# Cross-attention scores of the later blocks as three fp32r products, with the queries' lower parts on GpSimd

## The chip, the core and the metric

The kernel runs on one core of a Trainium2 chip. Its time is the device time of one execution in microseconds, as the median of the runs shown. Its engines are named as in the profile: PE is TensorE (matmuls; PEld are its weight loads), DVE is the Vector engine, ACT is ScalarE, POOL is GpSimd and SP is SyncE, which here only issues transfers.

## What is computed

One layer of a hybrid decoder for 1024 prompt tokens and 64 sample tokens (8 sequences of 8), all in float32: a feed-forward half step, a mixer of a recurrent and a sliding-window attention part, a cross attention over 256 memory tokens, a second feed-forward half step, and a final norm. The part that matters here is the cross attention, with 4 heads of width 256:

```
def cross_attend(h, mk, mv, w_cq, w_co):
    q = (h @ w_cq).reshape(n, t, X_HEADS, X_HEAD_DIM)
    s = jnp.einsum('nthd,nmhd->nhtm', q, mk) * (X_HEAD_DIM ** -0.5)
    p = jax.nn.softmax(s, axis=-1)
    o = jnp.einsum('nhtm,nmhd->nthd', p, mv).reshape(n, t, D_MODEL)
    return o @ w_co
```

The prompt tokens share one memory (`mk`, `mv`), each sample sequence has its own.

## The kernel before

Activations lie feature-major in SBUF: a tensor `[128, 8, T]` holds 1024 features as 8 tiles of 128 partitions, for T = 1088 tokens, the 64 of the samples first. Most products are made as three fp32r products: each operand is split into an upper part, rounded to fp32r, and a lower part, the operand less its upper part, and `three` (line 905) issues upper x upper, upper x lower and lower x upper into one PSUM bank. The products inside the attention are plain fp32 matmuls, each of which the trace shows as two instructions.

The weights of the five plain projections come as 27 pairs of tiles, of 128 x 1024 each. SP loads them (`load_pairs`), POOL splits each tile into an upper and a lower part in eight pieces of 128x256 (`split_plain`, lines 805 and 791 to 792), one pair after the other in `split_pairs` (line 835), and may overwrite `w_hi` and `w_lo` of a pair only when PE is through with the pair before it. Pairs 15 to 18 are the mixer's output projection, 19 to 22 the queries (`PAIR_CQ` = 19), 23 to 26 the cross attention's output projection (`PAIR_CO` = 23). POOL's program is one queue: line 882 runs the splits of pairs 18 to 26 in one loop, and after it the first weights of the second feed-forward part.

The cross attention runs in 8 steps, one for each block b of 128 prompt tokens and, at the same time, for sample sequence b. The order within a step is written out by hand on each engine, and semaphores tie them together:

- PE, `x_step(b)` (line 1483): the scores of block b+1 (`x_scores`, line 1425, into banks 0 and 1), the turn of block b's probabilities (`x_turn`, line 1453), the sample scores of b+1 (`y_scores`, line 1437), the turn of the sample's (`y_turn`), and the products with the values (`x_weigh`, lines 1471 and 1479). Step 0 is written out ahead of the loop, with `x_scores(0)` and `x_scores(1)` in the last tile of the query projection.
- DVE, `x_step(b)` (line 2878): the row maximum of b+1 (`x_soft`, lines 2855 to 2860), the copies of block b+2's queries into operands for PE (`x_stage`: `qs_b` on line 2850 and `xq_b` on line 2851, which raises `xq_st`), the normalization of b+1 (`x_norm`, lines 2864 to 2869), and the result of b out of PSUM (`x_take`).
- ACT, `x_step(b)` (line 1973): the turned probabilities out of PSUM, the exponentials of b+1 (`x_exps`, lines 1961 to 1964), and `y_s`, the sample's result, out of PSUM.
- SP loads the sample keys and values (`load_keys`, `load_values`), two sequences ahead, and the weights of pair 23 between the first of these.
- POOL has no part in a step. The split of pair 23 falls among the steps, because its weights come then.

`x_scores(b)` waits for `xq_st` at b+1 and `x_exp` at b+1. The keys `mem_kT` (128 x 8 x 256, fp32) were made by the memory projection long before.

Of the kernel before, what the change touches and what calls it, by code (L numbers as in the profile page):

```python
# [22 lines left out]
F32 = mybir.dt.float32  # L23
F32R = mybir.dt.float32r
ALU = mybir.AluOpType
ACT = mybir.ActivationFunctionType
AX_X = mybir.AxisListType.X

P = 128
D = 1024  # L30
KT = D // P
SEQ = 1024
NS, LS = 8, 8
TS = NS * LS
# [9 lines left out]
NB = SEQ // WIN  # L44
KVH = 2
GRP = NH // KVH
NM = 256
XH = 4
# [6 lines left out]
NC = len(CH)  # L55
# [65 lines left out]
PAIR_IN, PAIR_KV, PAIR_OUT, PAIR_CQ, PAIR_CO, PAIRS = 0, 7, 15, 19, 23, 27  # L121
# [84 lines left out]
def build(nc, t_in, t_out):  # L206
    ctx = ExitStack()
    with ctx:
        def sem(name):
            return ctx.enter_context(nc.semaphore(name))  # L210
# [5 lines left out]
        def at(name, shape, off, dt=F32):  # L216
            size = 4 * int(np.prod(shape[1:]))
            assert off % 32 == 0 and off + size <= LIMIT, (name, off, size)
            return nc.alloc_sbuf_tensor_at(name, shape, dt, offset=off)
# [120 lines left out]
        mem_kT = at("mem_kT", [P, KT, NM], P0 + M_G * ROW)  # L340
# [11 lines left out]
        def here(name, shape, dt=F32):  # L352
            off = cur[0]
            tns = at(name, shape, off, dt)
            cur[0] += -(-4 * int(np.prod(shape[1:])) // 32) * 32
            assert cur[0] <= (RS0 if off < RS0 else ACC0), name
            return tns
# [43 lines left out]
        xq = at("xq", [P, KT, T], P0 + 33792)  # L401
# [5 lines left out]
        qs_b = here("qs_b", [P, KT, 32])  # L407
# [8 lines left out]
        y_s = here("y_s", [P, NM])  # L416
        ck_T = [at("ck_T0", [P, KT, NM], ACC0), here("ck_T1", [P, KT, NM])]
        cv_n = [here(f"cv_n{s}", [P, 2, D]) for s in range(2)]

        y = at("y", [P, KT, T], A0)  # L420
        y_id = at("y_id", [P, P], A0 + KT * ROW)
# [2 lines left out]
        ps = ctx.enter_context(nc.psum_tensor("ps", [P, 8, 512], F32))  # L424
# [14 lines left out]
        memn_hi_done, memn_lo_done = sem("memn_hi_done"), sem("memn_lo_done")  # L439
# [62 lines left out]
        kw_hi_made = sem("kw_hi_made")  # L502
# [20 lines left out]
        ck_in = [sem(f"ck_in{s}") for s in range(2)]  # L523
        cv_in = [sem(f"cv_in{s}") for s in range(2)]
        xq_st = sem("xq_st")
        x_sc_mm, x_nmax, x_exp, x_p = sem("x_sc_mm"), sem("x_nmax"), sem("x_exp"), sem("x_p")
        x_turned = sem("x_turned")
        x_pt_mm, x_pt_ev, xp_ev = sem("x_pt_mm"), sem("x_pt_ev"), sem("xp_ev")
# [255 lines left out]
        def _(pool):  # L784
# [20 lines left out]
            def split_plain(s, p, hi=w_hi, lo=w_lo, less=0, both=True):  # L805
                pool.wait_ge(w_in[s], (p + 1) * 16)
                steps = Steps(pool, w_pool, p * (2 * KT // SHORT) + s * (KT // SHORT) - less * (KT // SHORT))
                split_short(w_raw[s], hi[s], lo[s], steps, w_split[s], both)
# [26 lines left out]
            def split_pairs(first, last, pair0, base, less=0):  # L835
                with pool.Fori(first, last) as p:
                    for s in range(2):
                        pool.wait_ge(w_mm[s], p * NC + (base - pair0 * NC))
                        split_plain(s, p, less=less)
# [31 lines left out]
            less = 2 * NB - 3  # L871
# [7 lines left out]
            for s in range(2):  # L879
                pool.wait_ge(w_mm[s], groups_before(PAIR_OUT + 1))  # L880
                split_plain(s, PAIR_OUT + 2, less=less)
            split_pairs(PAIR_OUT + 3, PAIRS, PAIR_OUT, 7 * NC, less=less)
            f = ffn["ffn2"]

            split_first(f)
# [2 lines left out]
            for c, (o, n) in enumerate(CH):  # L888
                for m in range(1, KT if c < NC - 1 else KT - 2):
                    i = c * KT + m  # L890
                    pool.wait_ge(sq_done, SQ0["final"] + i + 1)
                    if m == 1:
                        h = HALVES[0][0]
                        pool.tensor_tensor(acc[:, o:o + n], sq[:, h:h + n], sq[:, HALVES[1][0]:HALVES[1][0] + n],
                                           ALU.add).then_inc(sq_used, 2)
                    else:
                        h = HALVES[m % 2][0]
# [6 lines left out]
        def _(pe):  # L904
# [520 lines left out]
            def x_scores(b):  # L1425
                pe.wait_ge(xq_st, b + 1)
                pe.wait_ge(x_exp, b + 1)
                for h in range(XH):
                    for d in range(2):
                        pe.matmul(ps[:, h // 2, (h % 2) * NM:(h % 2 + 1) * NM], xq_b[:, 2 * h + d, :],  # L1430
                                  mem_kT[:, 2 * h + d, :], start=(d == 0), stop=(d == 1))

            def y_scores(b, half, s):
                pe.wait_ge(ck_in[s], half * 16 + 16)
                for h in range(XH):
                    for d in range(2):
                        ins = pe.matmul(ps[32 * h:32 * h + 32, 2, 0:NM], qs_b[:, 2 * h + d, :],
                                        ck_T[s][:, 2 * h + d, :], start=(d == 0), stop=(d == 1))
                ins.then_inc(x_sc_mm, 1)
# [7 lines left out]
            def x_turn(b, s):  # L1447

                pe.wait_ge(x_p, b + 1)
                pe.wait_ge(x_pt_ev, b + 1)  # L1450
                for h in range(XH):
                    for mt in range(2):
                        ins = pe.transpose(ps[:, 3 + mt, h * P:(h + 1) * P], xs_m[s][:, h, mt * P:(mt + 1) * P],
                                           x_id[:, :])
                ins.then_inc(x_turned, 1)

            def y_turn(b, s, after=True):

                if after:
                    pe.wait_ge(y_ev, b)  # L1460
                    back()
                for mt in range(2):
                    ins = pe.transpose(ps[:, 5, mt * P:(mt + 1) * P], ys_m[s][:, mt * P:(mt + 1) * P], x_id[:, :])
                ins.then_inc(x_pt_mm, 1)
# [17 lines left out]

            def x_step(b, half, s, more=True, after=True):
                if more:
                    x_scores(b + 1)
                x_turn(b, s)
                if more:
                    y_scores(b + 1, half + s, 1 - s)
                y_turn(b, s, after)
                x_weigh(b, half, s)  # L1490
# [34 lines left out]
        def _(act):  # L1525
# [432 lines left out]
            def x_exps(b, s):  # L1958
                act.wait_ge(x_nmax, b + 1)
                for h in range(XH):  # L1960
                    act.activation(xs_m[s][:, h, :], ps[:, h // 2, (h % 2) * NM:(h % 2 + 1) * NM], ACT.Exp,
                                   bias=xst[:, s, 1, h:h + 1], scale=XD ** -0.5, accum_out=xst[:, s, 2, h:h + 1])
                act.activation(ys_m[s][:, :], ps[:, 2, 0:NM], ACT.Exp, bias=yst[:, s * 4 + 1:s * 4 + 2],
                               scale=XD ** -0.5, accum_out=yst[:, s * 4 + 2:s * 4 + 3]).then_inc(x_exp, 1)
# [5 lines left out]
                    ps[:, 5, NM:2 * NM].rearrange("p (d w) -> p d w", d=2)[:, :, 0:P]  # L1970
                    .rearrange("p d (h w) -> p h d w", h=XH)[:, :, :, 0:LS], ACT.Copy)

            def x_step(b, s, more=True, after=True):

                act.wait_ge(x_turned, b + 1)
                act.activation(xp_T[:, :, :, :], ps[:, 3:5, :], ACT.Copy).then_inc(xp_ev, 1)
                act.wait_ge(x_pt_mm, b + 1)
                if after:
                    y_back(b - 1)
                act.activation(yp_T[:, :, :], ps[:, 5, 0:2 * P], ACT.Copy).then_inc(x_pt_ev, 1)  # L1980
                if more:
                    x_exps(b + 1, 1 - s)
                act.wait_ge(y_mm, b + 1)
                act.activation(y_s[:, :], ps[:, 5, NM:2 * NM], ACT.Copy).then_inc(y_ev, 1)

            act.sem_inc(x_exp, 1)
            act.sem_inc(x_pt_ev, 1)
            x_exps(0, 0)
            x_step(0, 0, after=False)
            x_step(1, 1)  # L1990
            with act.Fori(1, NB // 2 - 1) as i:
                x_step(i * 2, 0)
# [23 lines left out]
            for c, (o, n) in enumerate(CH):  # L2016
                for m in range(KT):
                    i, h = c * KT + m, HALVES[m % 2][0]
# [10 lines left out]
        def _(dve):  # L2029
# [815 lines left out]
            def xcol(b):  # L2845
                return bass.ds(b * P + TS, P)

            def x_stage(b):

                dve.tensor_copy(qs_b[:, :, :], xq[:, :, bass.ds(b * LS, 32)])  # L2850
                dve.tensor_copy(xq_b[:, :, :], xq[:, :, xcol(b)]).then_inc(xq_st, 1)

            def x_soft(b, s, steps):
                dve.wait_ge(x_sc_mm, b + 1)
                steps.mark(dve.tensor_reduce(xst[:, s, 0, :], ps[:, 0:2, :].rearrange("p a (h w) -> p (a h) w", w=NM),
                                             AX_X, ALU.max))
                steps.done(dve.tensor_reduce(yst[:, 4 * s:4 * s + 1], ps[:, 2, 0:NM], AX_X, ALU.max))
                dve.tensor_scalar(xst[:, s, 1, :], xst[:, s, 0, :], -(XD ** -0.5), None, ALU.mult)
                dve.tensor_scalar(yst[:, 4 * s + 1:4 * s + 2], yst[:, 4 * s:4 * s + 1], -(XD ** -0.5), None,
                                  ALU.mult).then_inc(x_nmax, 1)  # L2860
# [12 lines left out]
            def x_take(b):  # L2873
                dve.wait_ge(x_pv_mm, b + 1)
                take_out(xq[:, :, xcol(b)], ps[:, 6:8, :].rearrange("p a (k w) -> p (a k) w", w=P))\
                    .then_inc(x_o_ev, 1)

            def x_step(b, s, more=True, stage=True):
                if more:
                    steps = Steps(dve, x_own, (b + 1) * X_STEPS)  # L2880
                    x_soft(b + 1, 1 - s, steps)
                    if stage:
                        x_stage(b + 2)
                    x_norm(b + 1, 1 - s, steps)
                x_take(b)

# [196 lines left out]
```

## Time and profile before

| what | us |
|---|---|
| time, median of 3 runs | 2206.29 (2205.27 to 2209.5) |
| time of the profiled execution | 2212.15 |
| its span, first to last instruction | 2210.3 |
| PE busy | 2127.8 (96%) |
| DVE busy | 1593.4 (72%) |
| ACT busy | 775.1 (35%) |
| POOL busy | 514.1 (23%) |
| mean granted PE clock, share of full speed | 0.988 |

A row of the time-ordered view gives the start in us from the span's start, the duration in us, the engine, the line, the operation, output <- inputs, and how many instructions the row joins; in brackets stands how long the engine had been idle, and what ended it. A matmul's duration runs on while the next has begun, so PE's pace is read from the starts. A row of the grouped view gives the total busy time in us and the mean of one in ns.

### The profile page before, as it was taken

Reading aid. Unit: us, or ns where it says so; the run is one execution under the profiler, and the core shown is the slowest. Engines: PE = TensorE matmul, PEld = TensorE weight load, DVE = VectorE, ACT = ScalarE, POOL = GpSimd, SP = SyncE. Lnnn points to the kernel's source line nnn. Section 1 sums busy time; section 2 is a strip of 40 time slices with the busy share of each in tenths; the row PEclk is TensorE's granted clock in tenths of the full one; section 3 lists DMA queues with packets and bytes.
Section 4 is the critical chain, followed back from the end, with each engine's and each line's share of the span. In section 5 each row is a group of like instructions: output and inputs, shape, how many; then the busy total and the mean of one; then the engine's idle time right before and its main releaser. Section 6 shows DMA issues by size and latency. Waiting matters only on the chain. (4 is left out here: it accounts for less than half of the span.)

```text
span 2210.3 us, 39382 instructions
## 1 busy us (share of the span) xinstructions
PE 2127.8 (96%) x15452; PEld 2013.5 (91%) x15452; DVE 1593.4 (72%) x2283; ACT 775.1 (35%) x1348; POOL 514.1 (23%) x499
## 2 busy tenths in 40 slices
PE   6899999999999999989999999998999999999988
PEld 5799999999998888878898887988999999999987
DVE  7977878769789677899525155368778777696884
ACT  6422322333333415557312034154223223333332
POOL 1011111201000166779535321520111112010002
PEclk9999999999999999999999999999999999999999
DMA  3123232245633211243401062312232332456322
GB/s 140 68 99 128 95 131 109 107 163 226 251 113 130 104 64 39 66 145 102 169 29 59 20 248 77 137 40 74 93 128 101 125 112 104 168 221 250 117 108 82
DMA packets 77304, 261.91 MB, mean 118 GB/s; under 512 B 8711, under 2 KB 20999, under 8 KB 63623
## 3 DMA queue, kind: packets, MB, share of 16 engines
q1 hardware_dynamic: 74240, 256.98, 31.7%
q10 hardware_dynamic: 2951, 3.35, 0.5%
q8 instruction: 80, 1.31, 0.2%
q14 instruction: 33, 0.27, 0.0%
HBM read 186.21 MB, written 71.31 MB: 117 GB/s over the span
## 5 line engine op out<-in xcount | busy, mean ns | idle before, releaser
L910 PE MATMUL ps<-act_hi,op_hi 128*128 128x272 f32 x1712 | 495.9, 290 | 18.5 <-DVE sg L2170 5.8
L911 PE MATMUL ps<-act_lo,op_hi 128*128 128x272 f32 x1712 | 496.6, 290 | 0.0
L912 PE MATMUL ps<-act_hi,op_lo 128*128 128x272 f32 x1712 | 495.9, 290 | 0.0
L910 PE MATMUL ps<-t_hi,op_hi 128*128 128x272 f32 x1392 | 403.6, 290 | 8.7 <-DVE op_lo L2146 7.2
L912 PE MATMUL ps<-t_hi,op_lo 128*128 128x272 f32 x1392 | 403.0, 289 | 0.0
L911 PE MATMUL ps<-t_lo,op_hi 128*128 128x272 f32 x1392 | 402.8, 289 | 0.0
L910 PEld LDWEIGHTS ps<-act_hi,op_hi 128*128 128x128 f32 x1712 | 325.2, 190 | 22.2 <-issue 16.1
L1595 ACT ACTIVATE op_hi<-sums 128x512 fp32r<-128x512 f32 (+2 forms) x232 | 139.3, 601 | 553.2 <-DVE sums L2152 308.5
L818 POOL TENSOR_TENSOR hid_o<-hid_o 128x544 f32<-128x544 f32 x72 | 112.7, 1566 | 917.8 <-DMA hid<-hid_o 913.6
L911 PEld LDWEIGHTS ps<-act_lo,op_hi 128*128 128x128 f32 x1712 | 324.8, 190 | 0.0
L912 PEld LDWEIGHTS ps<-act_hi,op_lo 128*128 128x128 f32 x1712 | 324.7, 190 | 0.0
L910 PE MATMUL ps<-act_hi,w_hi 128*128 128x288 f32 (+1 forms) x864 | 292.0, 338 | 7.4 <-DVE act_lo L2072 2.0
L912 PE MATMUL ps<-act_hi,w_lo 128*128 128x288 f32 (+1 forms) x864 | 285.1, 330 | 0.0
L910 PEld LDWEIGHTS ps<-t_hi,op_hi 128*128 128x128 f32 x1392 | 263.6, 189 | 10.1 <-DVE op_lo L2146 7.8
L912 PEld LDWEIGHTS ps<-t_hi,op_lo 128*128 128x128 f32 x1392 | 263.8, 190 | 0.0
L911 PEld LDWEIGHTS ps<-t_lo,op_hi 128*128 128x128 f32 x1392 | 263.1, 189 | 0.0
L911 PE MATMUL ps<-act_lo,w_hi 128*128 128x288 f32 (+1 forms) x792 | 260.9, 329 | 0.0
L791 POOL TENSOR_TENSOR w_hi<-w_raw,ones 128x256 fp32r<-128x256 f32 x148 | 134.1, 906 | 511.7 <-DMA w_raw<-in_w_plain 287.6
L910 PEld LDWEIGHTS ps<-act_hi,w_hi 128*128 128x128 f32 x864 | 164.2, 190 | 25.5 <-issue 7.8
L912 PEld LDWEIGHTS ps<-act_hi,w_lo 128*128 128x128 f32 x864 | 164.3, 190 | 12.7
L792 POOL TENSOR_TENSOR w_lo<-w_raw,w_hi 128x256 fp32r<-128x256 f32 x172 | 161.1, 941 | 18.5 <-ACT w_hi L1825 6.9
L911 PEld LDWEIGHTS ps<-act_lo,w_hi 128*128 128x128 f32 x792 | 150.2, 190 | 13.2 <-issue 1.4
(352 smaller groups left out, 3943.5 us busy)
## 6 DMA issues: line engine op xcount, KB each, us to landing
raw_gu<-in_w_gu SPq DMA_DIRECT2D x40, 1024.0 KB, 6.0
w_raw<-in_w_plain SPq DMA_DIRECT2D x54, 512.0 KB, 3.3
hid<-hid_o SPq DMA_DIRECT2D x20, 1088.0 KB, 4.9
hid_t<-hid_o SPq DMA_DIRECT2D x18, 1088.0 KB, 4.0
hid_h<-sum_hi SPq DMA_DIRECT2D x16, 544.0 KB, 5.3
x<-x_keep SPq DMA_DIRECT2D x16, 544.0 KB, 6.2
raw_dq<-in_w_dq SPq DMA_DIRECT2D x8, 1024.0 KB, 5.9
ck_T<-in_ck SPq DMA_DIRECT2D x8, 1024.0 KB, 6.7
```

The lines of the kernel that those rows point to most:

```text
L791: steps.done(pool.tensor_tensor(hi[:, r, :], raw[:, r, :], one, ALU.mult))
L792: ins = pool.tensor_tensor(lo[:, r, :], raw[:, r, :], hi[:, r, :].bitcast(F32), ALU.subtract)
L818: pool.tensor_tensor(h[to], h[a], h[b], ALU.subtract).then_inc(f["t_made"], 1)
L910: pe.matmul(out, wh, ah, start=(first and n == 0), stop=False, skip_group_check=goes_on)
L911: pe.matmul(out, wh, al, start=False, stop=False, skip_group_check=goes_on)
L912: ins = pe.matmul(out, wl, ah, start=False, stop=end, skip_group_check=goes_on)
L1595: act.activation(hi, src, ACT.Copy).then_inc(f["w_hi"], 1)
```

## The change

From block 2 on the scores of the prompt tokens are made with `three`. The keys get an upper part `mk_hi`, made by ACT once in step 0, and a lower part `mk_lo`, made by POOL. DVE copies the queries of a block into `xq_hi` in place of `xq_b`, and POOL makes `xq_lo` from `xq` and `xq_hi`, once for each block from 2 to 7. POOL's loop of splits is cut in two: after pair 23 come `mk_lo` and the six `xq_lo`, and pairs 24 to 26 after them. PE waits for one more semaphore before the scores. Blocks 0 and 1 stay in fp32, as do the sample scores.

```diff
@@ -416,6 +416,8 @@
+        mk_hi, mk_lo = here("mk_hi", [P, KT, NM], F32R), here("mk_lo", [P, KT, NM], F32R)
+        xq_hi, xq_lo = here("xq_hi", [P, KT, P], F32R), here("xq_lo", [P, KT, P], F32R)
@@ -523,6 +525,7 @@
+        x_lo_done = memn_lo_done
@@ -879,7 +882,15 @@
-            split_pairs(PAIR_OUT + 3, PAIRS, PAIR_OUT, 7 * NC, less=less)
+            split_pairs(PAIR_OUT + 3, PAIR_CO + 1, PAIR_OUT, 7 * NC, less=less)
+            pool.wait_ge(kw_hi_made, 2 * NB - 2)
+            pool.tensor_tensor(mk_lo[:, :, :], mem_kT[:, :, :], mk_hi[:, :, :].bitcast(F32), ALU.subtract)\
+                .then_inc(x_lo_done, 1)
+            for b in range(2, NB):
+                pool.wait_ge(xq_st, b + 1)
+                pool.tensor_tensor(xq_lo[:, :, :], xq[:, :, b * P + TS:(b + 1) * P + TS],
+                                   xq_hi[:, :, :].bitcast(F32), ALU.subtract).then_inc(x_lo_done, 1)
+            split_pairs(PAIR_CO + 1, PAIRS, PAIR_OUT, 7 * NC, less=less)
@@ -1430,6 +1441,16 @@
+            def x_scores_split(b):
+                pe.wait_ge(xq_st, b + 1)
+                pe.wait_ge(x_lo_done, b + 1)
+                pe.wait_ge(x_exp, b + 1)
+                for h in range(XH):
+                    for d in range(2):
+                        t = 2 * h + d
+                        three(ps[:, h // 2, (h % 2) * NM:(h % 2 + 1) * NM],
+                              [(xq_hi[:, t, :], xq_lo[:, t, :], mk_hi[:, t, :], mk_lo[:, t, :])], d == 0, d == 1)
@@ -1482,7 +1503,7 @@
             def x_step(b, half, s, more=True, after=True):
                 if more:
-                    x_scores(b + 1)
+                    x_scores_split(b + 1)
                 x_turn(b, s)
@@ -1970,7 +1991,10 @@
+            def keys_hi():
+                act.activation(mk_hi[:, :, :], mem_kT[:, :, :], ACT.Copy).then_inc(kw_hi_made, 1)
+
-            def x_step(b, s, more=True, after=True):
+            def x_step(b, s, more=True, after=True, keys=False):
@@ -1980,13 +2004,15 @@
                 if more:
                     x_exps(b + 1, 1 - s)
+                if keys:
+                    keys_hi()
                 act.wait_ge(y_mm, b + 1)
@@
-            x_step(0, 0, after=False)
+            x_step(0, 0, after=False, keys=True)
@@ -2850,6 +2876,11 @@
+            def x_stage_hi(b):
+
+                dve.tensor_copy(qs_b[:, :, :], xq[:, :, bass.ds(b * LS, 32)])
+                dve.tensor_copy(xq_hi[:, :, :], xq[:, :, xcol(b)]).then_inc(xq_st, 1)
@@ -2880,7 +2911,7 @@
                     if stage:
-                        x_stage(b + 2)
+                        x_stage_hi(b + 2)
```

## Rows read from the trace of the kernel before

**Rows 1.** The page, busy us (share of the span) of each engine.

```profile
PE 2127.8 (96%) x15452; PEld 2013.5 (91%) x15452; DVE 1593.4 (72%) x2283; ACT 775.1 (35%) x1348; POOL 514.1 (23%) x499
```

**Rows 2.** Windows: busy us by engine in one steady step, then granted clock.

```profile
1306.90:1317.60 10.70, 10.70 (x96) 8.83 (x92) 5.42 (x12) 4.31 (x14) 0.00 (x0) 1.00 0.49 198
```

**Rows 3.** Time-ordered view, scores of blocks 2, 3, 4 and 7.

```profile
1284.59 3.72 PE L1430 MATMUL ps<-mem_kT,xq_b 128*128 128x256 f32 x16
...
1290.07 1.09 PE L1437 MATMUL ps<-ck_T,qs_b 128*32 128x256 f32 x16 [0.88 <-DMA ck_T<-in_ck]
...
1296.26 3.72 PE L1430 MATMUL ps<-mem_kT,xq_b 128*128 128x256 f32 x16
...
1299.60 1.01 PEld L1453 LDWEIGHTS ps<-x_id,xs_m 128*128 128x128 f32 x8
...
1300.78 0.61 PEld L1437 LDWEIGHTS ps<-ck_T,qs_b 128*32 128x32 f32 x16 [0.17 <-issue]
...
1301.97 1.23 DVE L2855 TENSOR_REDUCE xst<-ps 128x4 f32<-128x1024 f32 x1 [2.50 <-PE ps L1437]
...
1303.90 0.69 DVE L2851 COPY xq_b<-xq 128x1024 f32 x1
...
1306.96 3.72 PE L1430 MATMUL ps<-mem_kT,xq_b 128*128 128x256 f32 x16
...
1339.08 3.72 PE L1430 MATMUL ps<-mem_kT,xq_b 128*128 128x256 f32 x16
```

**Rows 4.** Time-ordered view of POOL: first, ninth and last piece of pair 23.

```profile
1286.34 0.73 POOL L791 TENSOR_TENSOR w_hi<-w_raw,ones 128x256 fp32r<-128x256 f32 x1 [34.91 <-DMA w_raw<-in_w_plain]
...
1292.29 0.73 POOL L791 TENSOR_TENSOR w_hi<-w_raw,ones 128x256 fp32r<-128x256 f32 x1
...
1299.00 0.72 POOL L792 TENSOR_TENSOR w_lo<-w_raw,w_hi 128x256 fp32r<-128x256 f32 x1
```

**Rows 5.** PE, memory projection: first of 24 matmuls and what follows; then loads, grouped.

```profile
1016.76 0.37 PE L910 MATMUL ps<-kw_hi,memn_hi 128*128 128x256 f32 x1
...
1019.67 0.60 PE L1206 MATMUL ps<-ident,s_m 128*128 128x128 f32 x4
...
L910 PEld LDWEIGHTS ps<-act_hi,w_hi 128*128 128x128 f32 x864 | 164.2, 190 | 25.5 <-issue 7.8
```

**Rows 6.** Time-ordered view of SyncE's queue: the issues around pair 23's weights.

```profile
1274.20 0.90 SPq L742 DMA_DIRECT2D cv_n<-in_cv  x2
1275.20 1.11 SPq L667 DMA_DIRECT2D w_raw<-in_w_plain  x2
```

**Rows 7.** POOL, 128x1024 operations at the kernel's start.

```profile
7.23 2.34 POOL L801 TENSOR_TENSOR c_hi_gate<-raw_gu,ones 128x1024 fp32r<-128x1024 f32 x1 [6.78 <-DMA raw_gu<-in_w_gu]
...
14.49 2.45 POOL L802 TENSOR_TENSOR c_lo_up<-raw_gu,c_hi_up 128x1024 fp32r<-128x1024 f32 x1
```

**Rows 8.** ACT, grouped by shape: a copy with fp32r output.

```profile
L1624 ACT ACTIVATE act_hi<-act_raw 128x2176 fp32r<-128x2176 f32 x6 | 12.1, 2020 | 3.1 <-DMA act_raw<-hid 3.1
```

**Rows 9.** PE after idle time: a window (clock 0.50), then matmuls behind block 7.

```profile
1060.00:1070.00 10.00, 9.73 (x43) 8.55 (x45) 0.21 (x1) 1.02 (x1) 9.45 (x14) 0.50 0.15 54
...
1360.62 0.44 PE L911 MATMUL ps<-act_lo,w_hi 128*128 128x288 f32 x1
...
1363.50 0.34 PE L911 MATMUL ps<-act_lo,w_hi 128*128 128x288 f32 x1
...
1363.82 0.29 PE L910 MATMUL ps<-act_hi,w_hi 128*128 128x288 f32 x1
1363.95 0.29 PE L911 MATMUL ps<-act_lo,w_hi 128*128 128x288 f32 x1
```

**Rows 10.** DVE's normalization beside POOL's split, and one block later alone.

```profile
1295.83 1.77 DVE L2866 TENSOR_TENSOR xs_m<-xs_m,xst 128x1024 f32<-128x1024 f32 x1
...
1296.60 1.59 POOL L792 TENSOR_TENSOR w_lo<-w_raw,w_hi 128x256 fp32r<-128x256 f32 x1
...
1306.51 1.22 DVE L2866 TENSOR_TENSOR xs_m<-xs_m,xst 128x1024 f32<-128x1024 f32 x1
```

## The prediction

> **What bounds the kernel now.** I read the page's busy shares first: TensorE (PE) is busy for 96% of the span [rows 1], so only what TensorE does or waits for can move the end. Then a table of busy time in windows cut at the cross-attention steps: in a steady step TensorE is busy for all of the 10.70 us, at a granted clock of 1.00, the Vector engine (DVE) for half of it, GpSimd (POOL) for nothing once its weight split is over [rows 2]. So each block's step lasts as long as TensorE's own instructions, and two things can change the time: fewer TensorE nanoseconds in a step, or something that TensorE must now wait for. Third, the time-ordered rows of one step [rows 3]: the scores start at 1296.26, the turn at 1299.60, the sample scores at 1300.78; DVE's maximum starts at 1301.97, its copy of the queries for the next scores at 1303.90, and these start at 1306.96. The copy is ready 2.4 us before TensorE comes to it: that is all the slack that a new operation between copy and scores has. Last, GpSimd's own rows around the change [rows 4]: idle 34.9 us until pair 23's weights land at 1286.34, then 16 pieces until 1299.7.
>
> **The scores on TensorE.** Removed for blocks 2 to 7: eight fp32 products, in the trace 16 instructions, from 1296.26 to the turn at 1299.60, so 3.35 us [rows 3]. Added: 24 fp32r matmuls of 128x256 with as many weight loads. The same shape stands in the memory projection: 24 of them from 1016.76 to the next instruction at 1019.67, 2.91 us [rows 5]. Gain 0.44 us a block. TensorE's work in a step becomes 10.71 - 0.44 = 10.27 us.
>
> **The queue that the keys' and queries' lower parts join.** This is the large term. `x_scores_split(2)` waits for `x_lo_done` at 3: the earlier count of 1, `mk_lo`, and `xq_lo` of block 2. Both stand in GpSimd's program behind `split_pairs(PAIR_OUT + 3, PAIR_CO + 1)`, whose last pair, 23, can't be split before its weights are there. SyncE issues that load at 1275.20, behind two transfers of sample values [rows 6], and it lands for GpSimd at 1286.34. In the kernel before nobody waits for this split (its user is the output projection), so it may end at 1299.7. Now the scores of block 2, which start at 1284.59 [rows 3], stand behind it. Step by step:
> - The split. Eight pieces run undisturbed from 1286.34 to 1292.29, 5.95 us [rows 4]; the later ones are stretched where DVE is at work. In the new kernel DVE has nothing after `x_take(0)` until the scores of block 2 are there, so all sixteen go at that pace: end at 1286.34 + 11.90 = 1298.24.
> - `mk_lo`, 128x2048. A 128x1024 operation on GpSimd takes 2.34 us [rows 7], a 128x256 piece 0.73 us [rows 4]: 0.19 us and 2.10 ns an element. For 2048 an estimate from these is 4.5 us; twice the 1024 row, 4.7 us, is the upper bound. With 0.1 us for the handover: 1302.8.
> - `xq_lo`, 128x1024 read in runs of 128 elements out of `xq`. The row for `c_hi_gate`, whose second operand is also walked in runs of 128, has 2.34 us, and the slowest of that group took 2.45 us [rows 7]. I take 2.35: end 1305.2, and with 0.1 us for the semaphore TensorE starts at 1305.4.
> TensorE is idle from 1284.59 to 1305.4: **+20.8 us**. No work can be done meanwhile, since all else of the step stands behind the scores in TensorE's program, and SyncE, ScalarE and DVE wait for TensorE in turn.
> - `mk_hi` on ScalarE, 128x2048 at about 1.9 us by the 128x2176 copy of 2.02 us [rows 8], comes in step 0 between the exponentials and the copy of `y_s`. It delays `y_s` of block 0, whose reader stands behind the scores that wait anyway, and it is done long before GpSimd asks for it. Nothing; without that cover up to 1.9 us once.
>
> **Restart at a lower clock.** After a gap TensorE comes back at half clock in this trace: after block 7's end the 288-column matmuls start every 0.24 us from 1360.62 to 1363.50 instead of every 0.13, and the stretch 1060 to 1070 was granted 0.50 for all its 10 us [rows 9]; that is 1.2 GHz instead of 2.4. In the first of these 12 steps lose 0.11 us each, about 1.5 us with the first one. The whole burst of 24 score matmuls at half clock would take 24 x 256 columns at 1.2 GHz, 5.1 us, instead of 2.91. I take this one burst, +2.2 us; bounds 1.5 us, and 5 us when the 10 us stretch repeats. Nothing gives it back, since the burst lies on the loop below. A rule of the Trainium skill speaks against the change here: "TensorE: Matmul & The Clock Gate", the section "Part 1: The HAM clock gate", has a long idle stretch put the array back to half clock. By it the sum has a term for the restart, without it the sum would be 2.2 us less; the rows above carry the term by themselves.
>
> **The loop of a later step.** From block 3 on, the queries' lower part lies on a ring: scores to turn 2.91 us, turn to sample scores 1.18, these to DVE's maximum 1.19, maximum to the start of the upper-part copy 1.93 [rows 3], the copy 0.69, a handover 0.1, `xq_lo` 2.35, a handover 0.1. Sum 10.45, say 10.5 us. That is above TensorE's own 10.27 and below today's 10.71. So TensorE should wait about 0.2 us a step for GpSimd, and half of the gain is lost. Two unknowns:
> - The copy now rounds to fp32r. No row has a one-input DVE operation with such an output. Bounds: 0.69 us as the plain copy [rows 3] and 1.22 us, the pace of one element a cycle [rows 10]. I take 0.69, since the operation, the shape and the width in bytes stay.
> - DVE's normalization and GpSimd's piece run at the same time. Where they meet in this trace they wait for each other: the 128x1024 multiplication took 1.77 us beside GpSimd's piece and 1.22 us alone, and the piece 1.59 instead of 0.73 [rows 10]. But `xq_lo` starts at 1304.7 in the frame of rows 3 and the multiplication at 1306.51, so it is DVE that waits, to about 1307.1. Its result is then there at about 1308.7, and the turn needs it at 1306.76 + 2.91 = 1309.7. Hidden, with 1 us left. The Trainium skill ("SBUF — State Buffer", "SBUF: two separate sides") calls this an exclusive lock which the first comer holds for its whole instruction; by a shared bandwidth instead, both would stretch and the ring would be some tenths longer. The rows agree with the lock.
>
> **The sum**, against the profiled execution (2212.15 us, span 2210.3, 5.9 us above the median of 2206.29): stall +20.8; first step (block 2's scores to block 3's) 11.67 before, with a wait of 0.88 us for the sample keys in it that the stall now covers, 10.5 after, -1.2; restart +2.2; four steps to block 7's scores at 10.5 instead of 10.71, -0.8; these scores themselves -0.4. Together +20.6: 2232.8 profiled, **2227 as a median**. Behind block 7 nothing absorbs it: the output projection's inputs come from this chain, and the feed-forward part is all TensorE.
>
> **The rivals.**
> - The ring is longer than I think, because the rounding copy runs at 1.22 us: 0.53 us in each of five steps, +2.7, 2230 us. For it: no row shows the form. Against: same operation and width.
> - The clock stays low for a whole step: nearly all of 10.3 us twice as long, about +8 instead of +2.2, 2233 us. For it: the 10 us stretch of rows 9, with transposes and small matmuls between products as here. Against: a dense burst of 3.3 us ended it at 1363.50.
> - The change's gain isn't there: 24 weight loads of 0.19 us each [rows 5] in a row, 4.56 us, become the bound of the scores, 1.65 us a block more than assumed, six blocks, +9.9, 2237 us. Against: such loads overlap in rows 5, where 24 fit into 2.91 us.
> - Not slower: there is no stall, because the pair-23 split is done in time. It decides at the landing of that load: for the scores to start at 1284.59 it must be there at 1284.59 - 2.45 - 4.6 - 11.9 = 1265.6. Then the time would be 2206.3 - 1.2 - 0.8 - 0.4, about 2204 us. Against it: the load is only issued at 1275.20 [rows 6].
>
> **How the numbers follow.** My forecast 0.65, the longer ring 0.14, the low clock 0.10, the weight loads 0.06, no stall 0.02, and 0.03 for a cause that I don't see. The likeliest case gives 2227, by its own bounds 2224 to 2230 (restart 1.5 or 3, `mk_lo` 4.4 or 4.7) and some 2 us more at each end, as the runs of before spread from 2205.3 to 2209.5. With the next two cases the range is 2222 to 2236. A measurement tells 0.2% (4.4 us) from no change; faster 0.01, same 0.02, slower 0.97.
>
> **What would show it.** The stall: a wait of about 21 us of TensorE at the first split scores, released by GpSimd's `xq_lo`; GpSimd's rows 16 split pieces, then 4.5 us for `mk_lo`, then 2.35 us. The gain: 24 matmuls within 2.9 us. The ring: starts of the scores 10.5 us apart, and a short wait on GpSimd before each; with 10.7 or more the ring or the copy was mis-sized, with 10.3 the ring isn't the bound. The restart: a granted clock of 0.5 for 3 to 6 us after the stall. The forecast is wrong if GpSimd's two pieces start ahead of the split, or if pair 23's weights land elsewhere than at 1286.

## The result, and the profile after

The changed kernel takes 2224.76 us as the median of 4 runs (2222.20 to 2225.32), the kernel before 2207.89 us in the same set of runs: a ratio of 1.0078, with a 95% interval of 1.0065 to 1.0090. A second set of runs (e8 below) gave 1.0071 (1.0058 to 1.0085). So the change costs 15.6 to 16.9 us by the medians, where 20.6 were forecast.

The page of the changed kernel against [rows 1]: TensorE has 8 us less to do and the span is 10 us longer. Both figures carry the chance of two single executions: of the 8 us only 1.6 lie in the part that the change touches (92.3 to 90.7 us busy between block 0's scores and the output projection), and the medians are 15.6 to 16.9 us apart, not 10.

```profile
span 2220.3 us, 39487 instructions
...
PE 2119.7 (95%) x15500; PEld 2008.6 (90%) x15500; DVE 1593.3 (72%) x2283; ACT 774.8 (35%) x1349; POOL 530.6 (24%) x506
```

The table of waits of TensorE around block 2 (what the engine waited for: total us, times, longest) has one line. It gives the releaser as "issue", that is, as nothing that the profile can name:

```profile
PE ps L921 <- issue: 20.5, 1, 20.5
```

GpSimd's time-ordered rows name it. They answer to [rows 4]; start, duration, operation, and in brackets the idle time before it:

```profile
1282.12 0.72 POOL L794 TENSOR_TENSOR w_hi<-w_raw,ones 128x256 fp32r<-128x256 f32 x1 [34.96 <-DMA w_raw<-in_w_plain]
...
1293.30 0.72 POOL L795 TENSOR_TENSOR w_lo<-w_raw,w_hi 128x256 fp32r<-128x256 f32 x1
1293.98 4.50 POOL L887 TENSOR_TENSOR mk_lo<-mem_kT,mk_hi 128x2048 fp32r<-128x2048 f32 x1
1298.43 2.34 POOL L891 TENSOR_TENSOR xq_lo<-xq,xq_hi 128x1024 fp32r<-128x1024 f32 x1
1310.45 2.37 POOL L891 TENSOR_TENSOR xq_lo<-xq,xq_hi 128x1024 fp32r<-128x1024 f32 x1 [9.67 <-DVE xq_hi L2882]
1320.70 2.37 POOL L891 TENSOR_TENSOR xq_lo<-xq,xq_hi 128x1024 fp32r<-128x1024 f32 x1 [7.88 <-DVE xq_hi L2882]
```

The split starts when its weights have landed, its sixteen pieces run without a break, the keys' lower part follows, then that of block 2's queries, until 1300.8. TensorE's rows, against [rows 3], take over there:

```profile
1279.35 1.07 PE L1500 MATMUL ps<-cv_n,yp_T 128*32 128x256 f32 x16
1300.88 0.55 PE L921 MATMUL ps<-mk_hi,xq_hi 128*128 128x256 f32 x1 [20.46 <-issue]
1301.23 0.41 PE L922 MATMUL ps<-mk_lo,xq_hi 128*128 128x256 f32 x1
1301.44 0.41 PE L923 MATMUL ps<-mk_hi,xq_lo 128*128 128x256 f32 x1
...
1305.60 1.03 PE L1474 MATMUL ps<-x_id,xs_m 128*128 128x128 f32 x8
...
1322.01 1.07 PE L1500 MATMUL ps<-cv_n,yp_T 128*32 128x256 f32 x16
1323.17 0.36 PE L921 MATMUL ps<-mk_hi,xq_hi 128*128 128x256 f32 x1
...
1326.12 1.04 PE L1474 MATMUL ps<-x_id,xs_m 128*128 128x128 f32 x8
...
1333.45 0.36 PE L921 MATMUL ps<-mk_hi,xq_hi 128*128 128x256 f32 x1
```

The last matmuls of block 0 start at 1279.35 and take 1.0 us, the scores of block 2 come at 1300.88: 20.5 us of idle TensorE. The first 24 matmuls then need 4.72 us until the turn at 1305.60: 18 start every 0.21 us and the last ones every 0.12. Those of a later block all start every 0.12 us and need 2.95. The windows show the clock beside it (busy us of each engine, then granted clock, in which 1.00 is 2.4 GHz and 0.50 is 1.2):

```profile
1280.40:1300.90 20.50, 0.04 (x4) 0.05 (x1) 2.32 (x3) 1.48 (x2) 18.03 (x18) 0.60 0.41 170
1300.90:1305.60 4.70, 4.70 (x25) 4.70 (x25) 0.00 (x0) 0.00 (x0) 0.00 (x0) 0.57 0.00 0
1323.10:1333.40 10.30, 10.16 (x100) 8.71 (x100) 5.85 (x12) 4.30 (x14) 2.38 (x1) 1.00 0.53 205
```

The third line answers to [rows 2]: a step now lasts 10.27 us (1323.17 to 1333.45), and TensorE is no longer busy all the time in it.

**Where the time went.** The two profiled executions differ by several us in stages that the change doesn't touch, so I compare a stretch: from the start of block 0's scores to the first product of the output projection. Every changed kernel that was run is in the table; e8 is the changed kernel a second time.

| kernel | scores of block 0 | first product | stretch | against before | whole kernel, ratio (95%) |
|---|---|---|---|---|---|
| before | 1262.97 | 1360.25 | 97.3 | | |
| changed | 1258.70 | 1374.53 | 115.8 | +18.5 | 1.0078 (1.0065 to 1.0090) |
| e1, queue order | 1260.43 | 1355.54 | 95.1 | -2.2 | 0.9984 (0.9972 to 0.9996) |
| e2, early load | 1263.33 | 1367.10 | 103.8 | +6.5 | 1.0021 (1.0009 to 1.0032) |
| e3, wait alone | 1263.41 | 1382.13 | 118.7 | +21.4 | 1.0098 (1.0073 to 1.0122) |
| e5, busy wait | 1258.96 | 1372.86 | 113.9 | +16.6 | 1.0078 (1.0056 to 1.0100) |
| e6, lower twice | 1260.63 | 1381.60 | 121.0 | +23.7 | 1.0108 (1.0094 to 1.0123) |
| e4, lower on DVE | 1257.46 | 1351.72 | 94.3 | -3.0 | 0.9982 (0.9973 to 0.9992) |
| e7, all of it | 1261.18 | 1354.39 | 93.2 | -4.1 | 0.9978 (0.9969 to 0.9987) |
| e8, changed again | 1258.83 | 1374.25 | 115.4 | +18.1 | 1.0071 (1.0058 to 1.0085) |

Within the stretch the changed kernel's +18.5 us is: the stall +20.5; block 2's scores to block 7's 53.1 instead of 54.5, -1.4 (the restart's +1.8 is in it); block 7's scores to the first product 20.5 instead of 21.2, -0.6.

### The profile page after: what moved, and what is told of

Its sections match the earlier page's. It is cut to its first block and busy times, and to the rows that moved or that the text cites. A ratio compares the mean times of both kernels' runs of the same rounds, so it can differ in the third digit from the quotient of the medians.

```text
span 2220.3 us, 39487 instructions
## 1 busy us (share of the span) xinstructions
PE 2119.7 (95%) x15500; PEld 2008.6 (90%) x15500; DVE 1593.3 (72%) x2283; ACT 774.8 (35%) x1349; POOL 530.6 (24%) x506
## 5 line engine op out<-in xcount | busy, mean ns | idle before, releaser
L921 PEld LDWEIGHTS ps<-act_hi,op_hi 128*128 128x128 f32 x1712 | 324.4, 189 | 20.6 <-issue 14.3
L795 POOL TENSOR_TENSOR w_lo<-w_raw,w_hi 128x256 fp32r<-128x256 f32 x172 | 160.4, 938 | 18.1 <-ACT w_hi L1846 6.5
L922 PEld LDWEIGHTS ps<-act_lo,w_hi 128*128 128x128 f32 x792 | 149.4, 189 | 13.3 <-issue 1.4
```

The costliest lines, as they stand in the source:

```text
L795: ins = pool.tensor_tensor(lo[:, r, :], raw[:, r, :], hi[:, r, :].bitcast(F32), ALU.subtract)
L921: pe.matmul(out, wh, ah, start=(first and n == 0), stop=False, skip_group_check=goes_on)
L922: pe.matmul(out, wh, al, start=False, stop=False, skip_group_check=goes_on)
```

## The experiments

**e1: the same work in another queue order.** ScalarE makes `mk_hi` right after block 0's exponentials. GpSimd, idle then, makes `mk_lo` and block 2's lower part ahead of pair 23's split, and block 3's between its two tiles. The first two hunks are GpSimd's program, the last is ScalarE's.

```diff
-            split_pairs(PAIR_OUT + 3, PAIR_CO + 1, PAIR_OUT, 7 * NC, less=less)
+            split_pairs(PAIR_OUT + 3, PAIR_CO, PAIR_OUT, 7 * NC, less=less)
...
             for b in range(2, NB):
...
+                if b < 4:
+                    s = b - 2
+                    pool.wait_ge(w_mm[s], groups_before(PAIR_CO))
+                    split_plain(s, PAIR_CO, less=less)
...
             x_exps(0, 0)
+            act.wait_ge(w_mm[1], groups_before(PAIR_CO))
+            keys_hi()
-            x_step(0, 0, after=False, keys=True)
+            x_step(0, 0, after=False)
```

> The change with another order in two queues, nothing else: ScalarE makes mk_hi as soon as the query projection is through (before step 0), and GpSimd makes mk_lo and the lower part of block 2 in its idle time ahead of pair 23's split, whose two tiles it splits after the lower parts of blocks 2 and 3. My theory (the queue alone costs the time): the stall of 20.5 us goes, with it the restart; the scores of block 2 start within 0.5 us of the kernel before; the steps stay at 10.27 us; about -2.2 us against the kernel before, so near 2205.7 us, ratio 0.999. Rival (the new operations themselves cost time: GpSimd's port shared with the Vector engine, ScalarE's extra copy, a GpSimd that is too slow for its split): part of the 17 us stays, the time is above 2212 us and waits on GpSimd show in several steps.

Measured: 2203.51 us against 2206.11 us, ratio 0.9984. GpSimd's rows:

```profile
1273.26 4.54 POOL L887 TENSOR_TENSOR mk_lo<-mem_kT,mk_hi 128x2048 fp32r<-128x2048 f32 x1 [24.38 <-ACT mk_hi L1999]
1279.99 2.37 POOL L891 TENSOR_TENSOR xq_lo<-xq,xq_hi 128x1024 fp32r<-128x1024 f32 x1 [2.19 <-DVE xq_hi L2888]
1283.84 0.74 POOL L794 TENSOR_TENSOR w_hi<-w_raw,ones 128x256 fp32r<-128x256 f32 x1 [1.48 <-DMA w_raw<-in_w_plain]
```

The scores of block 2 start at 1282.45, 22.0 us after those of block 0, as against 21.6 in the kernel before. The whole cost is gone, though every operation of the change is still there. The place in the queue made it, and the rival of the added work as such falls. (The stretch is even 2.2 us shorter than before, which is what the products bring less what the ring, explained below, takes.)

**e2: the queue order as changed, the weights earlier.** SyncE issues pair 23's load before it waits for the query projection's end.

```diff
+            load_pairs(PAIR_CO, PAIR_CO + 1)
             sp.wait_ge(w_mm[1], groups_before(PAIR_CO))
             load_keys(1, 1)
             load_values(0, 0)
             load_values(1, 1)
-            load_pairs(PAIR_CO, PAIR_CO + 1)
```

> The changed kernel with one move: SyncE issues the load of pair 23 before it waits for the end of the query projection. GpSimd's program order is as in the changed kernel. Theory: the first tile is split before the projection ends (it needs the weights' slot, free then), the second from about 1273.7 to 1279.7 in the time of the kernel before, mk_lo from 1285.9 (mk_hi comes then) to 1290.4, the lower part of block 2 until 1292.8; the stall shrinks from 20.5 to about 8.3 us and is then set by mk_hi, and the time falls by 12 us to about 2212.6 us. Rival (the stall is set by GpSimd's own new work, not by when the pair's weights land): no more than 2 us less than the changed kernel, above 2222 us.

Measured: 2211.89 us, ratio 1.0021.

```profile
1279.51 0.73 POOL L795 TENSOR_TENSOR w_lo<-w_raw,w_hi 128x256 fp32r<-128x256 f32 x1
1286.24 4.50 POOL L887 TENSOR_TENSOR mk_lo<-mem_kT,mk_hi 128x2048 fp32r<-128x2048 f32 x1 [6.00 <-ACT mk_hi L1995]
1290.70 2.34 POOL L891 TENSOR_TENSOR xq_lo<-xq,xq_hi 128x1024 fp32r<-128x1024 f32 x1
```

The stall is 8.2 us, where about 8.3 were worked out, and the rival (no more than 2 us less than the changed kernel) falls. The weights' landing set the long stall; with it out of the way GpSimd stands 6.0 us idle and waits for `mk_hi`, which ScalarE starts only at 1284.24. The forecast put that copy at no cost, with the stall as the work that hides it, and at up to 1.9 us, its own length, without that cover. What it cost here is not its length but the 6.0 us by which it comes late. Once the cover is thinner, the copy's place is the next thing that is late.

**e3: the wait without the products.** The scores stay in fp32 and DVE's copies plain ones; GpSimd makes `mk_lo` and one lower part, block 2's, and TensorE waits for that once.

```diff
-            for b in range(2, NB):
-                pool.wait_ge(xq_st, b + 1)
-                pool.tensor_tensor(xq_lo[:, :, :], xq[:, :, b * P + TS:(b + 1) * P + TS],
-                                   xq_hi[:, :, :].bitcast(F32), ALU.subtract).then_inc(x_lo_done, 1)
+            pool.wait_ge(xq_st, 3)
+            pool.tensor_tensor(xq_lo[:, :, :], xq[:, :, 2 * P + TS:3 * P + TS],
+                               xq_b[:, :, :], ALU.subtract).then_inc(x_lo_done, 1)
...
-                    x_scores_split(b + 1)
+                    if isinstance(b, int) and b == 1:
+                        pe.wait_ge(x_lo_done, 3)
+                    x_scores(b + 1)
...
-                        x_stage_hi(b + 2)
+                        x_stage(b + 2)
```

> The wait without the products: scores as before in fp32 from xq_b, mk_hi and mk_lo and one lower part (of block 2) are made in the changed kernel's places, and TensorE waits for that one before the scores of block 2; no lower parts later. Theory: the stall of 20.5 us, a restart at half clock of about 1.8 us and no gain, less the 0.9 us wait for sample keys that it covers: +21.4 us, about 2229.3 us, some 3 us above the changed kernel; steps of 10.71 us afterwards. Rival (the three fp32r products are no cheaper than the two-pass fp32 ones, and the stall is all): the same time as the changed kernel, 2224.8 us.

Measured: 2228.72 us, ratio 1.0098, and +21.4 us in the stretch.

```profile
1305.47 5.70 PE L1440 MATMUL ps<-mem_kT,xq_b 128*128 128x256 f32 x16 [20.24 <-POOL xq_lo L890]
1311.01 1.04 PE L1473 MATMUL ps<-x_id,xs_m 128*128 128x128 f32 x8
...
1328.86 3.72 PE L1440 MATMUL ps<-mem_kT,xq_b 128*128 128x256 f32 x16
1332.42 1.04 PE L1473 MATMUL ps<-x_id,xs_m 128*128 128x128 f32 x8
...
1339.57 3.72 PE L1440 MATMUL ps<-mem_kT,xq_b 128*128 128x256 f32 x16
```

Here the profile names GpSimd's lower part as the releaser. The fp32 scores take 3.56 us from their start to the turn (1328.86 to 1332.42), 5.54 us behind the stall, and a step is 10.71 us again. Between this kernel and the changed one lies what the fp32r products bring, less what the ring costs: 2.9 us in the stretch, 4 to 6.5 us in the medians. The two ratios' intervals overlap, so it is the trace that decides: the fp32r scores take 2.95 us to the turn and these 3.56. The rival of products that are no cheaper falls; the stall is what eats the gain.

**e5: TensorE kept busy in the stall.** 46 fp32 matmuls into bank 0 stand before the scores of block 2, which overwrite them.

```diff
+            def keep_warm():
+                pe.wait_ge(xq_st, 3)
+                pe.wait_ge(x_exp, 3)
+                for _ in range(46):
+                    pe.matmul(ps[:, 0, 0:NM], xq_b[:, 0, :], mem_kT[:, 0, :], start=True, stop=True)
```

> The changed kernel with 46 more fp32 matmuls of 128x256 (92 instructions, 19 us at 0.207 us each) into bank 0, issued while TensorE would be idle before the scores of block 2; their result is overwritten. Theory (the restart is paid because TensorE was idle): the scores of block 2 start at the same time but run at full clock, 2.95 instead of 4.72 us, and the time falls by 1.8 us to about 2223.0 us. Rival (the slow start has another cause, a first use of the new operands or the code of the loop): these 24 matmuls keep taking 4.7 us.

Measured: 2223.06 us. That is 1.7 us below the changed kernel's first median and 0.9 above its second, so the whole kernel's time can't decide between the two; the trace can.

```profile
1280.60 20.12 PE L1459 MATMUL ps<-mem_kT,xq_b 128*128 128x256 f32 x92
1300.97 0.36 PE L921 MATMUL ps<-mk_hi,xq_hi 128*128 128x256 f32 x1 [0.25 <-issue]
...
1303.92 1.04 PE L1481 MATMUL ps<-x_id,xs_m 128*128 128x128 f32 x8
```

The scores of block 2 start 0.1 us later than in the changed kernel and take 2.95 us instead of 4.72 (4.36 in e8, the changed kernel's second trace); the stretch is 1.9 us shorter. The slow start comes from the idle time, and not from a first use of the operands, which is the same here.

**e6: a dose for the ring.** The kernel of e1, with each lower part of the queries made twice and the scores waiting for the second (the last hunk is TensorE's wait).

```diff
+                for n in range(2):
+                    pool.wait_ge(x_lo_done, 2 + 2 * (b - 2) + n)
...
-                pe.wait_ge(x_lo_done, b + 1)
+                pe.wait_ge(x_lo_done, 2 * b)
```

> The version with the mended queue order, with every lower part of the queries made twice on GpSimd (the same result), the scores waiting for the second. A dose for the ring. Theory (the ring through GpSimd is as long as TensorE's work in a step or a little longer): each step grows by the whole 2.4 us, to about 12.7 us, in five steps, and block 2's scores start 2.4 us later: about 13.5 us more than the queue order alone, 2217 us. Rival (GpSimd has a reserve in a step, TensorE's work of 10.27 us bounds it): the reserve takes part of the 2.4 us; with 1 us of reserve the steps are 11.7 us and the time 2212 us.

Measured: 2229.53 us, ratio 1.0108: 26 us more than e1 (25.9 in the stretch), twice the 13.5 that I expected. The direction is the ring's, the size isn't. The time-ordered rows of one step, GpSimd's and DVE's:

```profile
1308.59 5.65 POOL L893 TENSOR_TENSOR xq_lo<-xq,xq_hi 128x1024 fp32r<-128x1024 f32 x2 [1.82 <-DVE xq_hi L2890]
...
1310.43 1.61 DVE L2905 TENSOR_TENSOR xs_m<-xs_m,xst 128x1024 f32<-128x1024 f32 x1
1311.96 2.42 DVE L2907 TENSOR_SCALAR ys_m<-ys_m,yst 128x256 f32<-128x256 f32 x1
```

And the window over the first 6 us of the step behind it, from the same kernel, columns as above:

```profile
1314.00:1320.00 6.00, 5.71 (x28) 5.71 (x29) 1.52 (x2) 0.00 (x0) 0.24 (x1) 0.53 0.62 259
```

First, the pair of lower parts takes 5.65 us, and not twice 2.37. The first piece ends at about 1311; DVE's normalization, which was waiting for it, goes next (1.61 instead of 1.23 us), the second piece waits for that, and DVE's next operation waits for the second piece (2.42 instead of 0.34 us). GpSimd and DVE take turns here, one instruction each, and the six pairs in the trace, one a block, all take 5.64 to 5.66 us. So the dose was 5.65 - 2.37 = 3.3 us. The step from 1300.76 to 1314.29, whose scores ran at full clock, is 13.53 us long, 3.26 more than 10.27: the whole dose appears, so GpSimd has no reserve in a step. Second, TensorE is idle for 3.3 to 3.6 us before each of the six split scores, and four of the six start at half clock: the line of the window has 0.53. The five steps were 14.85, 13.53, 15.90, 14.90 and 13.59 us. The sum closes: the dose six times is 19.6 us, the four slow starts take 1.3, 2.4, 1.4 and 2.3, and the wait of 1.1 us for block 2's sample keys is covered; together 25.9.

**e4: the lower parts on DVE.** The kernel of e1, with `xq_lo` made by DVE behind its copy.

```diff
                 dve.tensor_copy(xq_hi[:, :, :], xq[:, :, xcol(b)]).then_inc(xq_st, 1)
+                dve.wait_ge(xq_st, b + 1)
+                dve.tensor_tensor(xq_lo[:, :, :], xq[:, :, xcol(b)], xq_hi[:, :, :].bitcast(F32),
+                                  ALU.subtract).then_inc(x_lo_done, 1)
```

> The version with the mended queue order, and the queries' lower parts made by the Vector engine right behind the upper-part copy (1.22 us by the rows of its 128x1024 operations) in place of GpSimd (2.37 us and two handovers). Theory: in the changed kernel a step of 10.27 us holds a wait of about 0.17 us for GpSimd's lower part (the scores start 1.17 us after the sample products begin, 1.00 in the kernel before), so the steps become 10.10 us and the scores of block 2 start 0.3 us sooner: about 1.1 us less than with the queue order alone, ratio 0.998. Rival 1 (TensorE's own work is 10.27 us and the ring doesn't bind): steps of 10.27 us, the same time. Rival 2 (the Vector engine becomes late: its lower part pushes the normalization behind the turn): steps above 10.3 us and a wait of the turn on the normalized probabilities.

Measured: 2203.21 us against 2206.49 us, ratio 0.9982. Against e1's 0.9984 the times alone can't tell them apart; in the stretch e4 is 0.8 us shorter (1.1 expected), and its steps are 10.12 us. Both rivals fall with that, the one of steps that stay at 10.27 us and the one of a DVE that becomes late.

**e7: all of it.** e4 with e2's early load; GpSimd splits one tile of pair 23 before `mk_lo`, ahead of the steps, and the other after it. That second split doesn't stay clear of DVE's work, as I had expected it to: it runs from 1278.51 to 1286.98 in the steps of blocks 0 and 1, single pieces take up to 1.72 us, DVE's first `xq_lo` takes 1.63 us, and TensorE waits 0.50 us for it.

> All of it together: mk_hi before step 0, lower parts of the queries on the Vector engine, pair 23 loaded before the end of the query projection and split on GpSimd before and after mk_lo, outside the steps. Theory: besides the steps of 10.10 us, the sample keys of block 2 no longer queue behind the weights' transfer (a wait of 1.1 us in the mended order) and no split piece meets the Vector engine's work: about 1 us less than with the late load, near 2201.5 us, ratio 0.9975. Rival (the keys are late for their own transfer time): the wait for the sample keys at block 2 stays at 1 us and the time equals the one with the late load.

Measured: 2201.04 us, ratio 0.9978 (0.9969 to 0.9987), 0.22% below the kernel before and the lowest of all, though its interval overlaps those of e1 and e4. The wait for block 2's sample keys, 1.1 us in e1 and 1.2 in e4, is gone, so they were late behind the weights' transfer and not for their own length. A step in the windows:

```profile
1303.40:1313.50 10.10, 10.10 (x104) 8.70 (x100) 6.64 (x13) 4.30 (x14) 0.00 (x0) 1.00 0.55 209
```

and DVE's time-ordered rows in it:

```profile
1310.51 0.69 DVE L2884 CAST xq_hi<-xq 128x1024 fp32r x1
1311.23 1.23 DVE L2886 TENSOR_TENSOR xq_lo<-xq,xq_hi 128x1024 fp32r<-128x1024 f32 x1
1312.85 0.18 DVE L2900 RECIPROCAL xst<-xst 128x4 f32<-128x4 f32 x1 [0.40 <-ACT ys_m L1984]
1313.11 1.23 DVE L2902 TENSOR_TENSOR xs_m<-xs_m,xst 128x1024 f32<-128x1024 f32 x1
```

TensorE is busy for all of the step again. DVE's lower part fits between its copy and the end of the exponentials, for which it still waits 0.40 us, so the normalization isn't pushed back.

**e8: the changed kernel again,** unaltered.

> The changed kernel again, unaltered, in more rounds: its first comparison left 14 to 20 us. The two profiled executions, compared between the sample products of block 0 and the first product of the output projection, give +18.5 us, 1.5 us of it less than it would be because the output projection started at half clock in the profile before and at full clock in the profile after. If what lies around the changed stretch is the same in both, the ratio is 1.0084 to 1.0091, 2224.7 to 2226.3 us. If the first comparison's middle holds (1.0078), about 1 to 3 us are won elsewhere, outside the changed stretch.

Measured: ratio 1.0071 (1.0058 to 1.0085), 2222.19 us. The stretch in its trace is 1258.83 to 1374.25, +18.1 us. By the medians the whole kernel's difference is 1.6 and 2.5 us smaller than the stretch's, in the two sets of runs. That is no finding: the two intervals, 14.4 to 19.9 and 12.8 to 18.8 us, both contain the stretch's figure. The one profiled execution of before was a long one. The span behind the first product of the output projection is 850.1 us in it, 845.8 and 846.1 in the changed kernel's two, and 844.9 to 847.4 in all nine traces of changed kernels; the whole execution was 5.9 us slower than its kernel's median. So its long end looks like an accident of that execution, though one trace of before can't prove it. One part of it can be named: the output projection restarted at half clock there and in e1 (first product to second feed-forward part 97.1 us in both) and at full clock in the changed kernel's two traces (95.6).

## Why the forecast came out as it did, step by step

- **The stall: right, 20.5 us against 20.8.** Each of its terms held. Sixteen pieces end to end took 11.9 us (11.9), `mk_lo` 4.50 (4.5), `xq_lo` 2.34 (2.35), and TensorE started 0.1 us behind it (0.1). Of the 0.3 us, 0.1 is a handover that I put between two of GpSimd's own operations and that doesn't exist, and 0.1 is rounding in my sum (1302.84 + 2.35 + 0.1 is 1305.3, not 1305.4). e1 and e2 show that it is the place in the queue behind the load of pair 23, and nothing else of the change, that costs it.
- **No slower: fell.** That rival needed the weights by 1265.6, and its deciding point named only one of three things that have to be early. In e2 GpSimd splits the first tile from 1257.72 on, so those weights are early enough. But the second tile's slot is free only when the query projection ends (its first piece starts at 1274.23, behind a wait for TensorE), and `mk_hi` is there only at 1286.24. So TensorE is still held for 8.2 us. With `mk_hi` on time some 2.2 us would remain, by an estimate: 8.2 less the 6.0 us that GpSimd waits for it.
- **The restart: mechanism right, 1.8 us against 2.2.** I let the whole burst of 24 matmuls run at half clock; the last six ran at full clock (0.12 us apart from 1305.01 on). In the other traces with a long wait there the slow start cost 1.4 us (e8), 2.1 (e2, behind 8.2 us) and 2.0 (e3, fp32), so 1.8 us is one value out of a spread. e5 takes the idle time away and the slow start with it. The Trainium skill's rule in "TensorE: Matmul & The Clock Gate", section "Part 1: The HAM clock gate", fits this: the array came back at half clock after the stall and not after the same 20 us filled with matmuls. The rows from which I took the term were a poor ground for it: the slow restart behind block 7 in [rows 9] came after only 1.4 us of idle time, and behind the same wait eight of the ten traces came back at full clock. The 20 us of this stall are another case, and there the term held. The rival of a whole step at low clock fell: of a step of 12.04 us only the first 4 us were slow.
- **The products: right in sign, too small, 0.60 us a block against 0.44.** The step that failed is my reading of [rows 3]: I took the scores' end from the weight load of the turn (1299.60) before, and from a matmul's start in [rows 5]. From matmul to matmul it was 3.55 us before (3.56 in e3) and is 2.95 after. TensorE's own work in a step is therefore 10.12 us, as e4 and e7 show, and not the 10.27 of the forecast. The other rival, weight loads as the bound at 4.56 us, fell with that.
- **The ring: right in kind, 10.27 us against 10.45.** The same slip counted 0.2 us twice: the 2.91 us end at a matmul's start, the 1.18 us begin at the weight load 0.2 us before it. The terms as they came: scores to turn 2.95, to the sample scores 0.96, to DVE's maximum 1.19, to the copy 1.93, copy and handover 0.77, `xq_lo` and handover 2.48, sum 10.28. The wait for GpSimd is the 0.15 us between 10.27 and the 10.12 of e4 and e7. That it binds, and without reserve, is shown by e6 (longer, and each step longer by the dose) and e4 (shorter, and the steps shorter). My own sign would have misled here: "with 10.3 the ring isn't the bound" took TensorE's work as 10.27 us, so the measured 10.27 looks like TensorE's bound and is the ring's. That the two figures agree is chance. Five steps at 10.27 instead of 10.5 are the largest part of the 2.1 us by which the stretch came out below my 20.6.
- **The rounding copy: right.** It runs in 0.69 us, as "CAST", at the pace of the plain copy. The rival of 1.22 us fell.
- **DVE beside GpSimd: right where it was weighed, and used wrongly later.** In the changed kernel the normalization waits for the lower part (1.61 us instead of 1.22) and hides it. The Trainium skill's rule of an exclusive lock ("SBUF — State Buffer", "SBUF: two separate sides") agrees with that and with e6. It does not say which of two waiting operations goes next; e6 shows that DVE's goes between two of GpSimd's. In e6's expectation I left the lock out. It makes 0.9 us in each of six pairs (5.65 less twice 2.37), some 5 of the 12 us by which the expectation fell short; the other 7 are the slow starts, which I had not put in either.
- **The sum.** 18.5 us in the stretch, 20.6 forecast: 0.3 from the stall, 0.4 from the restart, 1.4 from the products and the ring. The whole kernel's medians give 15.6 to 16.9 us; the 1.6 to 2.5 us between them and the stretch are inside the intervals and stay without a cause.

## What to carry to other kernels

When an operation is appended to a queue, list what stands before it and when each of those can start; a queue whose work nobody waited for can be late by 20 us unseen, and the first critical wait put behind it pays for all of that. The profile's share of busy time is no guide there: GpSimd was idle for 35 us just before. And when a wait is made harmless, ask at once for the next link: here the weights, then the keys' upper part, which showed as a wait only when the weights were early.

## What the runs showed that I had not expected

- In all six pairs of e6 DVE and GpSimd alternated by the instruction while both had one ready. A second GpSimd operation issued right behind the first waited for the DVE operation between them (5.65 us for two of 2.37), and DVE's 0.34 us operation took 2.42.
- Repeated waits of 3.3 to 3.6 us of TensorE cost more than their length: behind four of six the clock was at half, which added about 1.3 to 2.4 us each time.
- For one and the same wait the profile names the releaser in one kernel and not in another: the 20 us for block 2's lower part are `POOL xq_lo` in e3 and "issue" in the changed kernel, and of e6's waits for the lower parts four are under `POOL xq_lo` (13.3 us) and two under "issue" (7.0 us). What decides it stays open. The other engine's rows around the end of the wait settle who released it.
